# A two-layer hybrid decoder trunk in f32: gates, branch outputs and their sum with tokens on partitions; the SSD rows loaded by ACT, the mask one addition, the sums a bias of the exponential

## The reference, cut to what matters

```
def segsum_exp(a_cs):
    L = a_cs.shape[-1]
    diff = a_cs[..., :, None] - a_cs[..., None, :]
    mask = jnp.tril(jnp.ones((L, L), dtype=bool))
    return jnp.exp(jnp.where(mask, diff, -jnp.inf))
...
    h = rmsnorm(x, norm_mix)
    q_a, k_a, v_a, q_b, k_b, v_b, z, xbc, dt_raw = split_cols(h @ w_in, IN_SIZES)
...
    gates = jax.nn.sigmoid((h @ w_gate + b_gate).astype(jnp.float32)).astype(x.dtype)
    g_a, g_b, g_c = jnp.split(gates, N_BRANCH, axis=-1)
    merged = g_a * (y_a @ w_br_swa) + g_b * (y_b @ w_br_moba) + g_c * (y_c @ w_br_ssd)
    x = x + merged @ w_mix_out
    hq = rmsnorm(x, norm_cross)
    hm = rmsnorm(mem, norm_mem)
...
    x = x + o @ w_co
    hf = rmsnorm(x, norm_mlp)
    return x + jnp.square(jax.nn.relu(hf @ w_up)) @ w_down
```

## Time and profile before

| | |
|---|---|
| median of three runs | 1178.68 us |
| profiled execution, its own time | 1178.97 us |
| its span | 1177.2 us |
| PE, DVE, ACT, POOL busy | 1166.1, 775.1, 596.3, 61.1 us |
| granted TensorE clock, mean | 0.999 |
| DMA | 201.31 MB, mean 171 GB/s |
| gate weights, issue to landing, median | 7.3 us |
| other weights | 5.0 to 5.4 us |
| row load `pT_sb<-acs_rows`, 256 KB | 4.9 us |
| ACT waited for gate weights | 27.5 us in 10 places |
| memory norm, high parts on ACT and low parts on DVE | 3.01 and 3.22 us |

### The profile page before, as it was taken

How to read it: one execution, slowest core, us unless ns; L and a number is a source line. 1 busy time by engine, 2 the same in 40 slices (tenths; PEclk the granted TensorE clock), 3 DMA queues, 4 the chain that set the end, 5 groups by cost and what they waited for, 6 DMA issues and landing times.

```text
span 1177.2 us, 18388 instructions
## 1 busy us (share of the span) xinstructions
PE 1166.1 (99%) x7491; PEld 1036.0 (88%) x7491; DVE 775.1 (66%) x1199; ACT 596.3 (51%) x870; POOL 61.1 (5%) x93
## 2 busy tenths in 40 slices
PE   8999999999999999999999999999999999999997
PEld 7988899999998888888889888999989988888886
DVE  7876856987455475665578677579775455766565
ACT  5656564445454354444455666453555444544443
POOL 1000003300000000000000000033000000000000
PEclk9999999999999999999999999999999999999999
DMA  7744426765644456556456443455755443755660
GB/s 238 237 143 132 156 85 187 220 213 176 194 143 151 136 180 204 188 180 199 159 156 205 144 144 108 140 172 191 250 179 180 144 143 111 244 182 180 202 208 37
DMA packets 156428, 201.31 MB, mean 171 GB/s; under 512 B 7168, under 2 KB 111928, under 8 KB 156344
## 3 DMA queue, kind: packets, MB, share of 16 engines
q1 hardware_dynamic: 155616, 199.58, 53.2%
q10 hardware_dynamic: 728, 0.55, 0.1%
HBM read 199.04 MB, written 1.08 MB: 170 GB/s over the span
## 4 chain that ended last, share of the span: by engine, by line
PE 94%; DMA 2%; DVE 1%; issue 1%; ACT 1%; POOL 1%; SPq 0%; POOLq 0%; DVEq 0%; ACTq 0%
PE psum L1153 12%; PE psum L1154 12%; PE psum L1155 12%; PE psum L1164 11%; PE psum L1165 10%; PE psum L1139 10%; PE psum L1167 10%; PE psum L1140 5%; PE psum L1186 1%; PE psum L1318 1%; PE psum L1356 1%; DMA raw<-in_w_gate_dram 1%; PE psum L1329 1%; PE psum L1374 1%; PE psum L1397 1%
## 5 line engine op out<-in xcount | busy, mean ns | idle before, releaser
L1499 DVE TENSOR_TENSOR w_lo<-raw,w_hi 128x2048 fp32r<-128x2048 f32 (+1 forms) x182 | 408.9, 2251 | 221.3 <-ACT w_hi L755 220.7
L755 ACT ACTIVATE w_hi<-raw 128x2048 fp32r<-128x2048 f32 (+1 forms) x182 | 341.6, 1879 | 158.2 <-PE psum L1167 109.6
L1153 PE MATMUL psum<-act_both,w_hi 128*128 128x256 f32 x832 | 241.0, 290 | 0.0
L1154 PE MATMUL psum<-act_both,w_hi 128*128 128x256 f32 x832 | 235.2, 283 | 0.0
L1155 PE MATMUL psum<-act_both,w_lo 128*128 128x256 f32 x832 | 235.2, 283 | 0.0
L1139 PE MATMUL psum<-act_both,w_hi 128*128 128x512 f32 x512 | 182.1, 400 | 0.0
L1153 PEld LDWEIGHTS psum<-act_both,w_hi 128*128 128x128 f32 x832 | 159.2, 191 | 4.1 <-issue 3.0
L1154 PEld LDWEIGHTS psum<-act_both,w_hi 128*128 128x128 f32 x832 | 159.3, 192 | 0.6 <-issue 0.5
L1155 PEld LDWEIGHTS psum<-act_both,w_lo 128*128 128x128 f32 x832 | 159.2, 191 | 0.0
L1140 PE MATMUL psum<-act_both,w_lo 128*128 128x256 f32 x512 | 143.7, 281 | 0.0
L1139 PEld LDWEIGHTS psum<-act_both,w_hi 128*128 128x128 f32 x512 | 96.2, 188 | 24.6 <-DVE act_both L1528 0.7
(11 more groups left out here) (261 smaller groups left out, 1928.2 us busy)
## 6 DMA issues: line engine op xcount, KB each, us to landing
raw<-in_w_in_dram SPq DMA_DIRECT2D x34, 1024.0 KB, 5.2
raw<-in_w_up_dram SPq DMA_DIRECT2D x32, 1024.0 KB, 5.4
raw<-in_w_down_dram SPq DMA_DIRECT2D x32, 1024.0 KB, 5.0
raw<-in_w_gate_dram SPq DMA_DIRECT2D x24, 1024.0 KB, 7.3
raw<-in_w_ckv_dram SPq DMA_DIRECT2D x16, 1024.0 KB, 5.3
raw<-in_w_br_ssd_dram SPq DMA_DIRECT2D x8, 1024.0 KB, 5.4
raw<-in_w_mix_out_dram SPq DMA_DIRECT2D x8, 1024.0 KB, 5.0
raw<-in_w_cq_dram SPq DMA_DIRECT2D x8, 1024.0 KB, 5.2
```

The costliest lines, as they stand in the source:

```text
L755: act.activation(w_hi[:, slot, 0:n], raw[:, slot, 0:n], ACT.Copy).then_inc(hi_ready.sem, 1)
L1153: pe.matmul(dst, m_hi[:, k, cs], a_hi[:, k, :], start=k == 0, stop=False)
L1154: pe.matmul(dst, m_hi[:, k, cs], a_lo[:, k, :], start=False, stop=False)
L1499: dve.tensor_tensor(w_lo[:, slot, 0:n], raw[:, slot, 0:n], w_hi[:, slot, 0:n].bitcast(F32), ALU.subtract).then_inc(lo_ready.sem, 1)
```

## The change

Units 21 to 40 go to orientation B: gates in stripes of 512 columns and two units, `branch_a` and `branch_b` in one unit each of 512 columns, `branch_c` in two stripes. `g_sb` and `mg_sb` have tokens on partitions. The gate's bias lies along the free axis now, so it is loaded as a broadcast row in halves (`bias_ab`, `bias_c`, SP), DVE adds it out of the bank (L1803 of the changed kernel), and ACT's Tanh works in place on `g_sb` (L831). The sum is turned by PE before the mix (`merged_turn`, behind unit 39 and in the middle of unit 41), its high and low parts are read from the bank, and the memory's norm is turned one unit later. The row loads of the SSD jobs are issued by ACT; the mask is one addition of 128x512 (L1868); the sums go into the exponential as a bias per partition (four activations of 128x128, L891). DVE makes the negated sums `neg_acs` once a layer.

```diff
-    stripes_a("gate", "w_gate", 0, "h", 4)
+    stripes_b("gate", "w_gate", 0, "h", 2)
     for j in range(2):
-        unit("branch_a", "A", "w_br_swa", 0, 4, 512 * j, 512, "y_swa", j)
-    stripes_a("gate", "w_gate", D, "h", 4)
+        stripe_b("branch_a", "w_br_swa", 512 * j, 512, "y_swa", j, (4,))
+    stripes_b("gate", "w_gate", D, "h", 2)
     for j in range(2):
-        unit("branch_b", "A", "w_br_moba", 0, 4, 512 * j, 512, "y_moba", j)
-    stripes_a("gate", "w_gate", 2 * D, "h", 4)
-    stripes_a("branch_c", "w_br_ssd", 0, "y_ssd", 4)
+        stripe_b("branch_b", "w_br_moba", 512 * j, 512, "y_moba", j, (4,))
+    stripes_b("gate", "w_gate", 2 * D, "h", 2)
+    stripes_b("branch_c", "w_br_ssd", 0, "y_ssd", 2)
...
-NORM_TURN_SLOT = {1: U_MIX, 2: U_QX - 2}
+NORM_TURN_SLOT = {1: U_MIX + 1, 2: U_QX - 2}
+MERGED_TURN_SLOT = (U_BRC + 2, U_MIX)
...
+                    for i, (slot, bias) in enumerate(((U_VB, bias_ab), (U_BRB - 1, bias_ab), (U_BRB + 3, bias_c))):
+                        if u in (slot, slot + 1):
...
+                            cs, c0 = slice(512 * (u - slot), 512 * (u - slot + 1)), D * i + 512 * (u - slot)
+                            sp.dma_start(bias[:, cs], a["b_gate"][l, c0:c0 + 512].partition_broadcast(P))\
+                              .then_inc(bias_loaded.sem, 16)
...
+                if kind == "gate":
+                    for t in range(TT):
+                        g = g_sb[:, t, 512 * j:512 * (j + 1)]
+                        act.wait_ge(*is_read(l, unit_bank(u, t)))
+                        act.activation(g, g, ACT.Tanh, scale=0.5).then_inc(gate_made.sem, 1)
+                    return
...
                 if branch == 2:
                     act.wait_ge(*decays_made.at(l, n - SSD_JOB0 + 1))
-                    act.activation(s_sb[:, n % 2, 0:512], s_sb[:, n % 2, 0:512], ACT.Exp).then_inc(exp_done.sem, 1)
+                    if n + 2 < NJOBS:
+                        spread(l, n + 2)
+                    for i in range(4):
+                        h, s = 4 * j + i, s_sb[:, n % 2, i * P:(i + 1) * P]
+                        ins = act.activation(s, s, ACT.Exp, bias=neg_acs[:, t, h:h + 1])
+                    ins.then_inc(exp_done.sem, 1)
                     return
...
+                    if u == job_slot(SSD_JOB0) - 1:
+                        act.wait_ge(*acs_stored.at(l, 16))
+                        for n in (SSD_JOB0, SSD_JOB0 + 1):
+                            act.wait_ge(*values_done.at(l, n - 1))
+                            spread(l, n)
...
+                        if w["act"] == "merged":
+                            part = w["row"] // 512
+                            pe.wait_ge(*mg_hi.at(l, 2 * part + t + 1))
+                            if part == 0:
+                                pe.wait_ge(*is_read(l, ("mergedT", 0, t)))
...
+            def merged_turn(l, j):
+
+                for t in range(TT):
+                    key = ("mergedT", j, t)
+                    pe.wait_ge(*mg_ready.at(l, 2 * j + t + 1))
+                    pe.wait_ge(*is_free(l, key))
+                    for k in range(4):
+                        c = 512 * j + k * P
+                        ins = pe.transpose(bank(key)[:, k * P:(k + 1) * P], mg_sb[:, t, c:c + P], ident[:])
+                    ins.then_inc(full(key), 1)
...
+                elif kind == "gate":
+                    branch, cs = w["col"] // D, slice(512 * j, 512 * (j + 1))
+                    dve.wait_ge(*bias_loaded.at(l, 32 * branch + 16 * (j + 1)))
+                    for t in range(TT):
+                        key = unit_bank(u, t)
+                        dve.tensor_tensor(g_sb[:, t, cs], bank(key), (bias_ab, bias_ab, bias_c)[branch][:, cs],
+                                          ALU.add).then_inc(free(key), 1)
...
-                    for i in range(4):
-                        h = 4 * j + i
-                        ins = dve.scalar_tensor_tensor(s_sb[:, n % 2, i * P:(i + 1) * P],
-                                                       pT_sb[:, n % 2, i * P:(i + 1) * P],
-                                                       acs[:, t, h:h + 1], mask_ssd[:], ALU.subtract, ALU.min)
-                    ins.then_inc(decays_made.sem, 1)
+                    dve.tensor_tensor(s_sb[:, n % 2, 0:512].rearrange("p (h k) -> p h k", k=P),
+                                      pT_sb[:, n % 2, :].rearrange("p (h k) -> p h k", k=P),
+                                      mask_ssd[:].unsqueeze(1).to_broadcast([P, 4, P]), ALU.add)\
+                       .then_inc(decays_made.sem, 1)
```

More of the change, by code:

```diff
@@ L248, in slot_banks @@
             out.append((YB_, ("closeT", i)))
+    if s in MERGED_TURN_SLOT:
+        out += [((TB_, OB_)[t], ("mergedT", MERGED_TURN_SLOT.index(s), t)) for t in range(TT)]
     for n in (1, 2):
@@ L471, in trunk @@
         acs_stored = Signal(sem("acs_stored"), 16)
-        acs_spread = Signal(sem("acs_spread"), 16 * 8)
+        acs_spread = [Signal(sem(f"acs_spread{i}"), 16 * 4) for i in range(2)]
         decays_made = Signal(sem("decays_made"), 8)
@@ L840, in evacuate @@
                            .then_inc(z_tanh.sem, 1)
-                elif kind == "gate":
-                    branch, tile = w["col"] // D, (w["col"] % D) // P
-                    if branch == 1:
-                        act.wait_ge(*is_read(l, (U_BRA + 1, 1)))
-                    if branch == 2:
-                        act.wait_ge(*is_read(l, (U_BRB + 1, 1)))
-                    for m in range(2):
-                        b0 = PC_BGATE + branch * KT + tile + m
-                        ins = act.activation(g_sb[:, tile + m, :], bank((u, 0))[:, m * SEQ:(m + 1) * SEQ],
-                                             ACT.Tanh, bias=half[:, l, b0:b0 + 1], scale=0.5)
-                    ins.then_inc(free((u, 0)), 1)
             def relu_high(l, j):
@@ L1015, in _ @@
                         norm_gain_hi(l, 3, ((0, 1), (2, 3))[u - U_CO - 2])
+                    for j in range(2):
+                        if u == MERGED_TURN_SLOT[j] + 1 - j:
+                            merged_hi(l, j)
                     evacuate(l, u)
@@ L1713, in evacuate @@
                     return
-                if not w["last"] or kind in ("qkb", "vb", "kx", "qx", "gate", "down"):
+                if not w["last"] or kind in ("qkb", "vb", "kx", "qx", "down"):
                     return
@@ L1792, in merged_lo @@
             def merged_lo(l, j):
[L1793 to L1796 removed]
+                for t in range(TT):
+                    key, ks, ts = ("mergedT", j, t), slice(4 * j, 4 * j + 4), slice(t * P, (t + 1) * P)
+                    dve.wait_ge(*mg_hi.at(l, 2 * j + t + 1))
+                    dve.scalar_tensor_tensor(act_lo[:, ks, ts], bank(key).rearrange("p (k n) -> p k n", n=P), 0.5,
+                                             act_hi[:, ks, ts].bitcast(F32), ALU.mult, ALU.subtract)\
+                       .then_inc(free(key), 1)
             def relu_low(l, j):
@@ L1943, in _ @@
                             close_lo_part(l, i)
+                    for j in range(2):
+                        if u == MERGED_TURN_SLOT[j] + 1 - j:
+                            merged_lo(l, j)
                     if 0 <= job_at(u):
```

105 lines of the change are left out of this document (54 added, 51 removed).

## The result

The changed kernel takes 1193.16 us, median of four runs (1191.73 to 1194.82), where the kernel before takes 1178.66 on the same chip: a ratio of 1.0122, interval 1.0109 to 1.0134. It is slower by 14.5 us. The profiled execution took 1192.92 us for a span of 1191.2 us, 14.0 us more than before by either.

The account below looks back on a forecast made before the run. PE bounds the kernel, with DVE only 2.1 us ahead at unit 37. Unit 43 comes 4.2 us later per layer, +8.4 us for two: 1178.97+8.4 = 1187.4, told as 1187 us; range 1172 to 1194, forecast's own 1180 to 1192.

Parts of the forecast that it names:

- The pauses of 2.4 us on DVE: Behind the bias additions at units 28, 30 and 34, DVE waits 2.4 us for ACT's second Tanh and high part.
- the waits of 1.3, 0.8 and 2.6 us: PE waits for DVE at the transpose behind unit 31, for unit 32's banks, and for unit 37's low part.
- The fourth: PE's wait at unit 33, which needs two free banks: PE would ask at 225.7 us and start at 231.0.
- Rival (1): DVE's pauses take up the new work and only PE's time counts: 1170.0 us, chance 0.20.
- Rival (2): DVE's meetings with POOL mostly go and PE waits for about what it gained: 1176 to 1181 us, chance 0.11.
- (3): Weights land late beside broadcasts and ACT's loads: 1191.4 us with one 2 us late per layer, 1195 with two; chance 0.07.
- (4): Matmuls of 512 columns take twice the 0.1199 us of 256, so the tiling saves nothing: 1189.9 us, chance 0.02.
- the walk: Layer 0, DVE's steps from unit 28's mask to unit 37's low part: done at 259.4 us, before 254.0.
- Now 7x0.317 = 2.2 us ahead: 199.4: The mask before unit 28's closing begins at 199.4 us instead of 201.58, because PE is 2.2 us ahead.
- The tiling on PE: Units of 24 matmuls instead of 48 save 0.317 us each on 40 units: -12.7 us of PE's work.
- Behind unit 37: To unit 43: -1.27 us for units 37 to 40, +0.93 for each of two turns, +0.3 waiting at unit 41.
- What I cost at nothing: Four-piece exponentials, ACT's row loads, loads off SP, bias broadcasts and the later memory norm were taken to add no time.

Follow-up runs that it names:

- experiment 8: The changed kernel with ACT's high part of the weights ahead of the gate's Tanh at unit 22 alone: 1191.15 us.
- experiment 3: The changed kernel with ACT making the high part of the weights three units ahead before the gate's Tanh, at every gate: 1172.90 us.
- experiment 4: The changed kernel with DVE's bias additions ahead of the closing instead of behind it at units 28, 30 and 34: 1177.61 us.
- experiment 7: The changed kernel with ACT's high part ahead of the gate's Tanh only at units 28, 30 and 34: 1174.80 us.
- experiment 9: The kernel before, with ACT's high part made to wait for DVE's closing at units 28, 30 and 34: 1188.26 us.
- experiment 1: The changed kernel with the old SSD part put back (SP's row loads, mask of four operations, one exponential): 1198.11 us.
- experiment 2: The kernel before with the SSD part of the change alone, without the tiling: 1178.93 us.
- experiment 5: The changed kernel with PE turning the identity into a bank of its own during four waits (units 31, 32, 33, 37): 1191.37 us.
- experiment 6: The changed kernel with ACT's high part ahead of every gate's Tanh and the old SSD part put back: 1178.52 us.
- experiment 10: The changed kernel with ACT's high part ahead of every gate's Tanh and DVE's bias additions ahead of closings at units 28, 30, 34: 1174.79 us.

## Why the prediction was right, and where it fell short

**The mechanism was right.** The pauses of 2.4 us on DVE at units 28, 30 and 34 are 2.50 us; the waits of 1.3, 0.8 and 2.6 us behind unit 31, at 32 and at 37 are 1.17, 0.80 and 2.64 us. The fourth does not fit: of the 5.3 us up to unit 33 the prediction left 3.2 for the wait there, and it was 1.42. PE came to unit 33 3.4 us later than forecast (1.03 us lost behind unit 23, 1.6 us at half clock in unit 32, 0.7 us less gain by the tiling), and DVE freed the banks only 1.6 us later. In experiment 8, without the first two, it is 3.05 us by starts:

```profile
231.54 0.47 PE L1188 MATMUL psum<-w_hi,act_both 128*128 128x512 f32 x1 [2.89 <-DVE tmp L1821]
```

Experiments 3, 4, 7 and 9 show the cause by taking it away in two ways, in three places alone, and by putting it into the kernel before. Rival (1), PE's work alone, is what experiment 3 is: 1172.9 us, not 1170.0. Rival (2) fell: masks still meet POOL three times ahead of unit 33 (1.77 to 1.79 us). Rivals (3) and (4) fell: gate weights land after 5.1 us (7.3 before) and ACT no longer waits for them, and matmuls start 0.227 us apart. The argument against (3), rows of 2 KB instead of 1 KB, wasn't the reason: with the old SSD part the gate weights take 7.3 us in rows of 1 KB (before) and 7.0 in rows of 2 KB (experiment 1), with the new one 5.2 (experiment 2) and 5.1 (the change). What differs is the row load of 256 KB that SP issues 0.4 us ahead of them in the old SSD part.

**The size was off by 6.2 us** between medians, so the forecast's own range (1180 to 1192 us) was missed, and the stated range held the result with 0.8 us to spare. Between the profiled executions it is 5.6 us, +14.0 where the sum had +8.4; the rest is how the two medians stand to them. The 5.6 us, term by term:

1. *Where the walk begins* (2.5 us). "Now 7x0.317 = 2.2 us ahead: 199.4" was wrong: the mask began at 200.66 us. From there each checkpoint was late by about the same amount, and the low part of 37 was there at 261.05 us for 259.4. Two causes. The same trap stands at unit 22, which I hadn't looked at, since no closing is there: DVE's pause there is 2.50 us too, and behind it stand the reading of PE's bank (L1977) and the denominators of job 15, so PE waits 1.03 us. And the tiling gave less (point 2). Experiment 8 moved the beginning by 1.09 us, and the end followed by 1.08. From the beginning to unit 37 the walk itself, 60.0 us by the sum, was 60.4 us: this is where pricing DVE, ACT and POOL from rows held. Unit 37 came 1.6 us later than forecast in layer 0 and 1.3 us in layer 1, so 0.4 us remain for the walk, in layer 0.

2. *The tiling on PE*. Inside a unit the 0.2266 us hold. But a unit gains 0.26 us (experiment 3, which waits nowhere: 4.76 us over 18 units), not 0.317. Behind each changeover the first matmuls start further apart with either size: it adds 0.07 to 0.09 us with 256 columns (the profile of before) and 0.10 to 0.14 us with 512 (experiment 3), and a piece in the middle of a unit makes a second changeover. That is 10.6 us for 40 units instead of 12.7. It counts where PE leads, hence in the beginning of the walk and in experiment 3; where DVE leads it costs nothing.

3. *TensorE's clock* (1.3 us in the profiled execution). Not in the sum at all; it assumed the 1.00 of the earlier trace rows. It fell in three stretches, and by experiment 5 the one behind unit 37 counts for 1.34 us; the other two each lie ahead of a wait. Experiment 5 shows that the stretches come with the idling, and experiment 9 that idling brings one into the kernel before. The Trainium skill (TensorE: Matmul & The Clock Gate, "A second HAM failure mode: psum-queue depth-cycling") tells of a kernel in which PE idled briefly but often between groups of matmuls and the clock went to and fro between its two levels; the trace agrees that such waits can bring the clock down, but here a few single waits were enough.

4. *The end* (0.9 us). From the scaling of the last output to the end of the span it is 3.6 us before and in experiments 1, 2 and 6, but 4.5 us in the change and experiments 3, 4 and 7: with tiling and SSD part together, not with either alone. Why is open; ACT's output DMA takes 2.9 instead of 2.5 us to land. No run was made on it.

5. *Behind unit 37*: +0.89 us forecast to unit 43; in layer 1 it was +0.91. The turning of the sum was priced rightly. The rest, some 0.4 us, is in small changes between the stages.

**What I cost at nothing**: experiment 2 bears it out for the kernel before, and no row load or broadcast shows in PE's waits. But taking the row loads off SP was not worth nothing everywhere. With the tiling and the old SSD part (experiments 1 and 6) ACT waits for gate weights again, 18.8 and 42.7 us, and the mask of unit 28 in layer 0 meets POOL, 1.92 and 1.94 us instead of 0.69. The whole SSD part is worth 4.9 and 5.6 us there; what the mask has of it is not shown.

By the 2.5 ns of the Trainium skill (TensorE: Matmul & The Clock Gate, "Wait — 56ns, not 53.3ns?") the tiling in experiment 3 would have given 2.4 us instead of 10.6, and 1181 us, an estimate; it ended at 1172.9. Its other statement there, that at 1.2 GHz matmuls start exactly 426.7 ns apart for 512 columns, agrees with the 0.425 us of the slow stretches.

## What to carry to other kernels

When a change puts a second engine into a hand-over, write down for every place where it occurs what stands behind the waiting instruction, not only where the work is dense: here the same pause stood at a fourth place, and it moved the beginning of everything that followed. If an engine has been idle before a wait (ACT 7.4 us), move the work that others need ahead of it before giving up the change; that turned +14.5 us into -5.8 us. And weigh an edit in the kernel that it will stand in: the SSD part was worth nothing until PE had moved forward.

## What the runs showed of the hardware that was not expected

Behind waits of PE of 0.8 to 3.0 us the granted clock fell to half, in some places and not in others: in the change's profile at unit 37 in layer 0 (260.6 us) but not in layer 1. The kernel before, whose clock is full until PE's work is over, has such a stretch once it is made to wait (experiment 9: from 824.7 to 828.1 us, behind a wait of 1.5 us). In the profiles of experiments 7, 9 and 10 there is one at the launch too, which begins at some 9 us, behind waits of 0.8 to 1.0 us. The wait of 1.0 us at unit 23, with full work around it, brought it in none of the profiles. Filling the waits with 46 transposes of the identity a layer, some 0.11 us each, took all such stretches away (experiment 5) and cost 0.15 us at unit 37. In the profile of experiment 8 one of 6.8 us (817.3 to 824.1) stood in layer 1 in place of PE's wait at unit 37: time lost to the clock and time lost to a wait take each other's place, and don't add up.
